# Router stages of a two-layer decoder step, without nine products that nobody reads

## What is computed

```python
def _hier_moe(u, rg_w, rg_b, re_w, re_b, w1, w3, w2):
    t = u.reshape(b_sz * seq_len, d)
    g_prob = jax.nn.softmax((t @ rg_w + rg_b).astype(F32), axis=-1)
    g_val, g_idx = lax.top_k(g_prob, 1)
    e_logits = (t @ re_w + re_b).astype(F32).reshape(-1, N_GROUPS, EXPERTS_PER_GROUP)
    e_logits = jnp.take_along_axis(e_logits, g_idx[:, :, None], axis=1)[:, 0]
    e_prob = jax.nn.softmax(e_logits, axis=-1)
    e_val, e_idx = lax.top_k(e_prob, EXPERT_TOPK)
    weights = g_val * e_val / jnp.sum(e_val, axis=-1, keepdims=True)
    ...
    h1 = jnp.einsum('td,edf->tef', t, w1)
    h3 = jnp.einsum('td,edf->tef', t, w3)
    act = jax.nn.silu(h1) * h3 * combine[:, :, None].astype(t.dtype)
    y = jnp.einsum('tef,efd->td', act, w2)
```

## Time and profile before

| | us |
|---|---|
| median of three runs | 1086.38 |
| lowest and highest | 1084.44, 1086.89 |
| the profiled execution | 1092.19 |
| its span, first to last instruction | 1090.2 |
| mean granted clock of PE in it | 0.967 |

### The profile page before, as it was taken

One profiled execution on the slowest core, in us unless ns is written; L12 is line 12 of the kernel. 1 busy time (PEld: TensorE's weight loads), 2 busy tenths in 40 slices (PEclk: granted clock), 3 DMA queues, 4 the chain that ended last, 5 costly groups with the idle time before them and its releaser, 6 DMA issues.

```text
span 1090.2 us, 13265 instructions
## 1 busy us (share of the span) xinstructions
PE 1022.5 (94%) x5408; PEld 575.1 (53%) x5408; DVE 344.0 (32%) x888; ACT 159.1 (15%) x298; POOL 39.8 (4%) x70
## 2 busy tenths in 40 slices
PE   7999999999799999999988998999999998889996
PEld 3666655584466554444445355777655444443533
DVE  3231133236333451111110058557461111110036
ACT  2200000004222110000000030073110000000021
POOL 0000000002300000000000200000000000000020
PEclk9999999969799999999999999999999999999897
DMA  9835677819963429999999971324519999999941
GB/s 377 355 141 223 245 288 278 346 43 372 407 250 147 162 86 402 423 422 422 421 423 421 419 294 65 142 106 164 234 46 372 415 421 422 422 422 422 407 167 49
DMA packets 47912, 317.30 MB, mean 291 GB/s; under 512 B 5634, under 2 KB 6034, under 8 KB 12642
## 3 DMA queue, kind: packets, MB, share of 16 engines
q1 hardware_dynamic: 39456, 288.90, 65.6%
q0 software_dynamic: 6384, 23.35, 5.8%
q10 hardware_dynamic: 2002, 4.08, 1.0%
HBM read 303.84 MB, written 12.47 MB: 290 GB/s over the span
## 4 chain that ended last, share of the span: by engine, by line
PE 72%; DMA 20%; DVE 5%; issue 2%; SPq 0%; ACT 0%; DVEq 0%
PE banks L775 25%; DMA scr<-in_ew 19%; PE banks L1384 13%; PE banks L1431 5%; PE banks L1354 4%; PE banks L854 4%; PE banks L894 2%; PE banks L841 1%; PE banks L1396 1%; PE banks L1363 1%; PE banks L963 1%; DMA ring<-in_w 1%; PE banks L786 1%; PE banks L862 1%; PE banks L1122 1%
## 5 line engine op out<-in xcount | busy, mean ns | idle before, releaser
L1384 PE MATMUL banks<-scr 128*64 128x512 f32 x512 | 116.9, 602 | 24.3 <-DMA scr<-in_ew 24.3
L775 PE MATMUL banks<-uT,ring 128*128 128x320 f32 x448 | 124.5, 438 | 3.2 <-DVE uT L1634 3.2
L1431 PE MATMUL banks<-ring,scr 128*64 128x512 f32 x512 | 116.2, 606 | 1.7 <-issue 1.7
L1384 PE MATMUL banks<-ring,scr 128*64 128x512 f32 x512 | 113.4, 593 | 3.4 <-issue 3.4
L775 PEld LDWEIGHTS banks<-uT,ring 128*128 128x128 f32 x448 | 85.5, 192 | 43.7 <-issue 8.4
L1354 PEld LDWEIGHTS banks<-scr 128*128 128x128 f32 x768 | 89.0, 193 | 13.5 <-issue 11.6
L1354 PE MATMUL banks<-scr 128*128 128x128 f32 x768 | 92.9, 278 | 0.3 <-DVE scr L1826 0.3
L1384 PEld LDWEIGHTS banks<-scr 128*64 128x64 f32 x512 | 38.3, 138 | 100.9 <-issue 63.0
L1384 PEld LDWEIGHTS banks<-ring,scr 128*64 128x64 f32 x512 | 37.9, 137 | 76.3 <-issue 74.1
L1431 PEld LDWEIGHTS banks<-ring,scr 128*64 128x64 f32 x512 | 36.1, 139 | 68.1 <-issue 66.7
L775 PE MATMUL banks<-ring,uT 128*128 128x512 f32 x128 | 58.7, 612 | 0.0
(11 more groups left out here) (385 smaller groups left out, 1053.4 us busy)
## 6 DMA issues: line engine op xcount, KB each, us to landing
ring<-in_ew SPq DMA_DIRECT2D x128, 1024.0 KB, 18.3
ring<-in_w SPq DMA_DIRECT2D x80, 1024.0 KB, 8.1
scr<-in_ew SPq DMA_DIRECT2D x64, 1024.0 KB, 21.1
yd<-scr POOLq DMA_DIRECT2D x14, 512.0 KB, 8.4
scr<-in_v POOLq DMA_DIRECT2D x16, 256.0 KB, 9.7
scr<-in_kT POOLq DMA_DIRECT2D x13, 256.0 KB, 9.0
out_hgrn<-scr SPq DMA_DIRECT2D x1, 2304.0 KB, 18.3
scr<-in_s POOLq DMA_DIRECT2D x1, 2048.0 KB, 9.0
```

The costliest lines, as they stand in the source:

```text
L775: last = mm(out, a, b, start=(first and i == 0), stop=(final and i == len(pairs) - 1))
L1384: ins = mm(ps[bank][SLOTS * x:SLOTS * x + SLOTS, :], xe[:, kk, SLOTS * x:SLOTS * x + SLOTS], wab[SLOT[n]][:, x, kk % 4, :], start=(kk == 0 ...
L1431: ins = mm(ps[5 + c][SLOTS * x:SLOTS * x + SLOTS, :], actT[:, f, SLOTS * x:SLOTS * x + SLOTS], wab2[SLOT[n]][:, x, f % 2, 512 * c:512 * c ...
```

## The change

The function `idle` and its four calls are taken out: four products ahead of step 4 of `tokens`, two ahead of the wait for `sel_ready`, one behind the counts, and two between the first gather and the wait for `over_ready`. That makes nine in each layer. Nothing is added or moved.

```diff
-            def idle(n):
-
-                for _ in range(n):
-                    give(mm(ps[7][:, :], ident, const[:, 0:512], start=True, stop=True))
-
             def slots(l):
 
                 lr_turn(l)
                 for n in range(6):
-                    if n == 4:
-                        idle(4)
                     tokens(l, n)
-                idle(2)
                 pe.wait_ge(sem("sel_ready"), l + 1)
...
                     .then_inc(sem("pos_ps"), 1)
-                idle(1)
...
                 slots(l)
                 gather(l, 0, 0)
                 gather(l, 0, 1)
-                idle(2)
                 pe.wait_ge(sem("over_ready"), l + 1)
```

## The result

The changed kernel takes 1091.78 us at the median of six runs, the kernel before 1084.54 us at the median of its six. The ratio is 1.0071, with a 95% interval of 1.0044 to 1.0097: slower by 7.7 us (4.8 to 10.5). Forecast were +3.4 us and 1089.8. A second measurement beside the experiments gave 1.0079 (1.0051 to 1.0108). So the sign was right, and the size came out at somewhat over twice the forecast. All ratios here leave out rare executions of 1190 us and more (three of the 24 of `no_four` and `filled`, three of the kernel before beside them).

A forecast was written before the change was run, and what follows sets the result against it. The start of L1384 was taken to set the weight stream and layer's end. Direct saving 0 plus slower small products, 2 x 1.7 = +3.4 us, on 1086.4 gave 1089.8 us; range 1085.5 to 1096.2.

The forecast's parts named there:

- The bound: Expert stages: they wait for the weight stream, so moving L1384's start moves the layer's end by the same amount.
- The direct saving: Removing the nine fillers per layer saves 0 directly, as they lie beside waits or the branch; at most 1.72 us per layer.
- on the path: Rival: fillers behind the gather delay L1384, so removal gains 1.72 us per layer, 3.4 in all: 1083.0 us; chance 0.11.
- The small products: The 18 small count products (L775) run at the low clock and delay DVE's L1762: +1.7 us per layer.
- hidden: Rival: the 18 count products don't slow, or the clock holds; no change, 1086.4 us; chance 0.21.
- The gather: First gather, 48 records, 5.62 us at full clock: slows but stays covered by the branch, costing nothing unless cold throughout.
- the first case: Clock comes back 3.4 us into the first gather, which then takes 7.3 us and ends at 396.6 us.
- cold throughout: Rival: first gather stays at low clock and L1384 starts cold, 4.9 us per layer: 1096.2 us; chance 0.21, one layer included.
- The start of L1384: Experts' first products: a clock fall in the gap before them costs 1.7 us, equally likely before and after; taken as nothing.

The follow-up runs named there:

- no_four: Kernel before with only the four fillers ahead of step 4 of `tokens` taken out; ratio 1.0031 (0.9998 to 1.0064), +3.4 us.
- filled: Kernel before with five fillers instead of four ahead of step 4 of `tokens`, four instead of two behind the gather; ratio 1.0030, +3.3 us.
- late_start: Kernel before with ten fillers instead of two between the first gather and the branch; ratio 1.0128 (1.0094 to 1.0162), +13.9 us.
- tail_off: Kernel before with only the two fillers between the first gather and the branch taken out; ratio 1.0044 (1.0017 to 1.0072), +4.8 us.
- tail_only: Kernel before with the seven fillers in the slots taken out, the two behind the gather kept; ratio 1.0058 (1.0032 to 1.0084), +6.3 us.

## Why the prediction was right, and where its size was off

**The bound.** Right. The start of L1384 sets the weight stream and the layer's end; `late_start` shows that a delay there arrives whole, and perhaps more than whole.

**The direct saving.** Right at zero. The four sets of fillers lay beside waits or beside the branch; `tail_off` has no earlier start without them. The rival "on the path" holds only behind a slow gather, as in layer 1 of `tail_only`, and there for some 0.5 to 0.7 us.

**The small products.** Right: forecast +1.7 us per layer, measured +1.5 (2.26 to 3.83 us; 0.1 hid behind DVE). The factor is 1.69, not L963's 1.84. The rival "hidden" falls. The page "TensorE: Matmul & The Clock Gate" of the Trainium skill, section "LDWEIGHTS (loading the stationary operand)", gives one time for a weight load, its columns over 1.2 GHz, with no second case for the other level of the clock. These traces disagree: the records of the same loads of 128 columns are 190 ns long at 1.00 and 326 ns at 0.50.

**The gather.** Right: 7.05 and 7.59 us, close to the 7.3 of the first case and far from 9.0, and beside the branch. The rival "cold throughout" did not come, but one part of its price, the cold start of L1384, came without it. The cover was not quite whole: the experts start 0.15 and 0.54 us later after over_i, for which I had nothing. The branch took 3.7 to 3.8 us, and in layer 1 the load came 0.6 us after over_i was begun.

**The start of L1384.** Here the step failed. I had priced a fall there at 1.7 us, which is what it costs (+1.70, +1.69), and then took nothing, since it was "about as likely before as after". It was not as likely. I had looked at layer 0 alone: the gap in front of the experts was 2.33 us there but 1.10 in layer 1, and without fillers it is 2.77 and 2.52, longer than my 0.7 to 2.4. In 15 layers with wide fillers behind the gather, over all traces, the experts' first 32 records never started at the low clock; 13 of their gaps were 1.9 us or less, and the other two 2.32 and 2.33. In 11 layers without them, or with narrow ones, the gaps were 2.21 to 4.25 us, and 9 started cold. Those that did not had 2.21 and 2.51. This term, 2 x 1.7, is what the sum lacks: 3.4 + 3.4 = 6.8, measured 7.1 in the routers and 7.7 in the time.

These 26 layers don't separate the length of the gap from the work in front of it, since the fillers change both. The expert stages do. There PE waits for weights behind products of 512 columns. In the 13 traces, the clock was at 1.00 behind all 116 waits of 1.2 to 1.91 us, and fell behind 7 of 9 waits of 1.92 to 2.08 us and behind 19 of 31 of 2.26 to 2.67 us. So wide products in front of a gap do not protect it, and two gaps of 2.3 us behind fillers are too few to say that fillers do. Two waits of the same length behind the same products, the first pair from the kernel before and the second from `tail_only`, where 16 of the 32 records follow at once:

```profile
986.50 7.05 PE L1384 MATMUL banks<-ring,scr 128*64 128x512 f32 x32
996.07 8.78 PE L1384 MATMUL banks<-scr 128*64 128x512 f32 x32 [2.51 <-DMA scr<-in_ew]
```

```profile
989.11 7.04 PE L1380 MATMUL banks<-ring,scr 128*64 128x512 f32 x32
998.66 3.65 PE L1380 MATMUL banks<-scr 128*64 128x512 f32 x16 [2.50 <-DMA scr<-in_ew]
```

What decides between two such gaps no run here shows. My own had a cold start behind 2.51 us, so a price of nothing for a gap of 2.4 us was not founded on the rows.

That the predicted time of 1089.8 us is within 2 us of the measured one is in part luck: the median of the kernel before had fallen from 1086.38 to 1084.54 with more runs, which hid some of the missing term. The difference is the fairer test, and there I was at 3.4 for 7.7.

## What to carry to other kernels

A product whose result nobody reads may be what keeps the products around it fast. Before such fillers are taken out, look for the small products behind them that stand on another engine's path, price those at both levels of the clock, and do the same for the first products of the next heavy stage. Whether a gap can cost a cold start is read from gaps of its own length elsewhere in the trace, in every layer, and it is a matter of how often and not of yes or no.

A branch on a computed value can cover products that are issued in front of it. How much it covers is read from the sequencer's own rows, and here the cover got shorter when those products ran slowly or were more: the load of over_i came 0.3 and 0.6 us after over_i was begun in the changed kernel, and 1.5 and 2.9 us in `late_start`.

## What the runs showed of the hardware that I had not expected

Gaps of PE between wide products cost nothing up to 1.91 us (0 of 116), and from 1.92 to 2.67 us they cost a cold start in 26 of 40 cases, with no order by length within that range. Products of 64 columns, issued back to back for 5.5 us, lost the clock in 5 layers of 22, in traces of both kernels. And fillers that start at 0.50 can be worth their place: behind two of them, 3.54 us long, the clock was up again for the small products, which were slow in every layer whose slots had no wide fillers.
